# Seven block products in place of eight in the second layer's FFN input, from the ninth pair on

## What is computed

```
def swiglu(h, w_in, w_out):
    g, u = jnp.split(h @ w_in, 2, axis=-1)
    return (jax.nn.silu(g) * u) @ w_out
...
        fl = swiglu(rms_norm(xl, g_ffn_pre[i]) * (1.0 + sc2) + sh2, w_ffn_in[i], w_ffn_out[i])
        xl = xl + gt2 * rms_norm(fl, g_ffn_post[i])
```

## Time and profile before

| | us |
|---|---|
| median of 3 runs | 1643.54 (1643.48 to 1644.06) |
| the profiled execution, whole | 1640.58 |
| its span | 1638.8 |
| first half of the FFN input (11 pairs) | 1265.9 to 1391 |
| first half of the output product | 1391.4 to 1451 |
| second half of the FFN input (11 pairs) | 1451 to 1571 |
| second half of the output product and the end | 1571 to 1638.8 |

### The profile page before, as it was taken

One profiled execution on the slowest core, in us unless ns is written; L12 is line 12 of the kernel. 1 busy time (PEld: TensorE's weight loads), 2 busy tenths in 40 slices (PEclk: granted clock), 3 DMA queues, 4 the chain that ended last, 5 costly groups with the idle time before them and its releaser, 6 DMA issues.

```text
span 1638.8 us, 25486 instructions
## 1 busy us (share of the span) xinstructions
PE 1592.5 (97%) x9666; PEld 1362.3 (83%) x9666; DVE 871.4 (53%) x1488; ACT 684.6 (42%) x1289; POOL 413.8 (25%) x311
## 2 busy tenths in 40 slices
PE   6999999999899999999999999999999999999998
PEld 4878887678899999997887788888887888888886
DVE  5856567718888878868777420136845331011103
ACT  4242226827544444433336441248855322222322
POOL 2311232035000000000002242325433444444442
PEclk9999999999999999999999999999999999999999
DMA  9743111023244334438964536224012543333322
GB/s 358 268 132 90 40 27 53 2 78 90 84 138 143 123 118 143 123 126 292 352 252 143 167 120 139 80 86 106 15 67 62 173 123 100 107 102 91 99 95 76
DMA packets 176360, 204.07 MB, mean 125 GB/s; under 512 B 16664, under 2 KB 138864, under 8 KB 175856
## 3 DMA queue, kind: packets, MB, share of 16 engines
q1 hardware_dynamic: 162232, 156.62, 30.6%
q10 hardware_dynamic: 14008, 45.83, 8.8%
HBM read 187.97 MB, written 12.88 MB: 123 GB/s over the span
## 4 chain that ended last, share of the span: by engine, by line
PE 89%; DVE 4%; ACT 3%; DMA 1%; issue 1%; POOL 1%; SPq 0%; DVEq 0%; ACTq 0%; POOLq 0%
PE ps L2508 28%; PE ps L2555 25%; PE ps L3063 18%; PE ps L2875 3%; PE ps L2818 3%; PE ps L2781 3%; PE ps L2738 2%; PE ps L2664 1%; PE ps L2759 1%; PE ps L2625 1%; PE ps L2537 1%; DMA mod_early<-in_w_mod 1%; DVE prob L1837 1%; ACT junk L1153 1%; ACT prob L1337 1%
## 5 line engine op out<-in xcount | busy, mean ns | idle before, releaser
L641 POOL TENSOR_TENSOR w_lo<-w_raw,w_hi 128x1024 fp32r<-128x1024 f32 (+1 forms) x122 | 299.5, 2456 | 577.6 <-ACT w_hi L1166 577.6
L1166 ACT ACTIVATE w_hi<-w_raw 128x1024 fp32r<-128x1024 f32 (+1 forms) x202 | 211.9, 1051 | 193.9 <-PE ps L2555 166.3
L2508 PE MATMUL ps<-h_hi,w_hi 128*128 128x512 f32 (+1 forms) x768 | 254.9, 367 | 1.1 <-DVE h_lo L1714 1.1
L2508 PE MATMUL ps<-h_hi,w_lo 128*128 128x512 f32 (+1 forms) x768 | 252.9, 365 | 0.0
L2508 PE MATMUL ps<-h_lo,w_hi 128*128 128x512 f32 (+1 forms) x768 | 251.7, 363 | 0.0
L2508 PEld LDWEIGHTS ps<-h_hi,w_hi 128*128 128x128 f32 x768 | 133.8, 189 | 27.4 <-issue 2.1
L2508 PEld LDWEIGHTS ps<-h_lo,w_hi 128*128 128x128 f32 x768 | 133.2, 189 | 23.2
L2508 PEld LDWEIGHTS ps<-h_hi,w_lo 128*128 128x128 f32 x768 | 133.4, 189 | 22.9
L641 DVE TENSOR_TENSOR w_lo<-w_raw,w_hi 128x1024 fp32r<-128x1024 f32 x77 | 93.8, 1221 | 98.0 <-ACT w_hi L1166 97.8
L3063 PE MATMUL ps<-hc_hi,h_hi 128*128 128x384 f32 x420 | 141.7, 337 | 2.4 <-ACT x_u L1214 2.4
L3063 PE MATMUL ps<-hc_hi,h_lo 128*128 128x384 f32 x420 | 141.0, 336 | 0.0
(11 more groups left out here) (353 smaller groups left out, 3036.5 us busy)
## 6 DMA issues: line engine op xcount, KB each, us to landing
w_raw<-in_w_ffn_in SPq DMA_DIRECT2D x88, 512.0 KB, 3.8
w_raw<-in_w_ffn_out SPq DMA_DIRECT2D x66, 512.0 KB, 3.5
mod_raw<-in_w_mod ACTq DMA_DIRECT2D x38, 512.0 KB, 5.5
mod_early<-in_w_mod SPq DMA_DIRECT2D x30, 512.0 KB, 9.7
w_raw<-in_na_w_in SPq DMA_DIRECT2D x29, 512.0 KB, 3.7
gate_b<-in_w_mod ACTq DMA_DIRECT2D x18, 512.0 KB, 4.6
hid_far<-full SPq DMA_DIRECT2D x22, 384.0 KB, 2.3
xs<-hid_far SPq DMA_DIRECT2D x22, 256.0 KB, 6.0
```

Source lines behind the costliest of these rows:

```text
L641: eng.tensor_tensor(w_lo[:, ring(u), 0:width], w_raw[:, u % RAW, 0:width], w_hi[:, ring(u), 0:width].bitcast(F32), ALU.subtract).then_inc( ...
L1166: act.activation(w_hi[:, ring(u), 0:width], w_raw[:, u % RAW, 0:width], ACT.Copy).then_inc(w_hi_done, 1)
L2508: mm = pe.matmul(o[0], sta(x, o), mov(y, o), start=first and n == 0, stop=last and n == 2)
```

## The change

The first eight pairs of the first half stay as they are. Pairs 9 to 11 of the first half and all eleven of the second (14 pairs, numbered n = 0 to 13 in `QN`) are computed with seven products, each of 4 blocks of 128 features x 3 matmuls, with 256 columns moving. The tokens are split into two halves of 256 and the features into two halves of 512, which gives the activation blocks. What is new or moved:

- `quick_t_sums` makes the four sums of activation blocks (VectorE, during the first pair), from the unrounded activations, which now stay in `y_half` (`full_of`); `quick_t_high` and `quick_t_low` split them (pairs 2, 3, 6, 7).
- For each of the 14 pairs: `quick_sum` makes the four sums of weight blocks (VectorE, 512 columns each), `quick_high` (ScalarE) and `quick_low` (VectorE) split them two at a time (1,024 columns each), and the u unit's second block A22 alone is split as before: high part by ScalarE, low part by GpSimd, 512 columns. The g unit's low part moves to VectorE (`by_dve`), but for n = 0 and n = 3.
- `quick_product` on TensorE, in the order P5, P7, P2, P1, P3, P4, P6. P3 waits until ScalarE has copied P5's bank, P4 until VectorE has added P7's bank to that copy, P6 until VectorE has added P1's bank and the copy of P2's.
- `raw_free` holds back the load into a slot until the pair's last sum (S4) is made too.
- The multiplication silu(g) u writes `hid_raw1`; low parts of the hidden values are made after the stage's last pair (first half) or at its end (second half), since the output product needs them only then.
- Sums and plans of the last modulation vector come one pair earlier.

The core of the diff:

```diff
+    quick_g = [sp(("fi1L", half)) + 2 * j for half, j in QN]
+    quick_u = [g + 1 for g in quick_g]
+    for n, g in enumerate(quick_g):
+        if n not in (0, FH - QUICK):
+            by_dve[g] = True
...
+            if v in quick_g or v in quick_u:
+                eng.wait_ge(*quick_summed((quick_g if v in quick_g else quick_u).index(v), "s4"))
...
+            def quick_in(half, first, hooks):
+
+                s = sp(("fi1L", half))
+                for j in range(first, FH + 1):
+                    n = QN.index((half, first)) + j - first
+                    if j > first:
+                        d = quick_banks(n - 1)[2]
+                        dve.wait_ge(f_u, Q_U + n)
+                        dve.tensor_tensor(quad[:, QW:3 * QW].rearrange("p (a n) -> p a n", a=2), PS[:, d:d + 2, 0:QW],
+                                          bass.AP(q_u.tensor, q_u.offset, [list(q_u.ap[0]), [0, 2], [1, QW]]),
+                                          ALU.add).then_inc(f_12, 1)
+                        dve.tensor_tensor(quad[:, 3 * QW:], q_u, q_t, ALU.add).then_inc(f_22, 1)
+                    if j < FH:
+                        quick_low(n, 1)
+                    if j > first:
...
+                        dve.tensor_tensor(hid_raw1[:, (j - 1) * SEQ:j * SEQ], quad[:, 0:2 * QW], quad[:, 2 * QW:],
+                                          ALU.mult).then_inc(hid_made, 1)
+                    if j < FH:
+                        dve.wait_ge(s_used, Q_USED + 3 * n + 2)
+                        dve.wait_ge(fp_copied, Q_COPIED + 2 * n + 1)
+                        dve.tensor_tensor(q_t, quick_ps(quick_banks(n)[3]), q_part, ALU.add).then_inc(f_t, 1)
+                        feed(s + 2 * j + 1)
+                        if j + 1 < FH:
+                            quick_sum(dve, n + 1, "s1")
+                            quick_sum(dve, n + 1, "s3")
+                        dve.wait_ge(w_used, ring_no[s + 2 * j] + 1)
+                        dve.wait_ge(fp_copied, Q_COPIED + 2 * n + 2)
+                        dve.tensor_tensor(quad[:, 0:QW], quick_ps(quick_banks(n)[0]), q_two, ALU.add).then_inc(f_11, 1)
+                        if j + 1 < FH:
+                            quick_low(n + 1, 0)
+                            quick_sum(dve, n + 1, "s2")
+                            quick_sum(dve, n + 1, "s4")
+                        feed(s + 2 * j + 2)
...
+                for j in range(first, FH):
+                    n = QN.index((half, j))
+                    for p in (5, 7, 2, 1, 3, 4, 6):
+                        quick_product(n, p)
```

More of the change, by code:

```diff
@@ L53 @@
 PARTS = HALF // P
+QUICK = 8
+QN = [(0, j) for j in range(QUICK, FH)] + [(1, j) for j in range(FH)]
+QW = SEQ // 2
 FAST_JOBS = ("s1", "s3", "s4", "a22", "s2")
@@ L272, in build @@
         by_dve[u] = True
+    quick_g = [sp(("fi1L", half)) + 2 * j for half, j in QN]
[3 more added lines that the diff above has]
+            by_dve[g] = True
+    for half in range(2):
+        by_dve[sp(("fo1L", half))] = True
     ups = range(sp("fi0") + 3, sp("fi0") + 2 * FT, 2)
@@ L306, in build @@
         gate_b = sb("gate_b", [P, 2, D])
+        with ExitStack() as early:
+            s42 = sb("s42", [P, 2, UNIT], F32R, scope=early)
         xs = sb("xs", [P, 2, D])
+        with ExitStack() as early:
+            t4_lo = sb("t4_lo", [P, 4, QW], F32R, scope=early)
         full = sb("full", [P, KT, P])
@@ new lines, in unit_cols, with quick_banks, quick_ps, quick_slot @@
+        def unit_cols(u):
+            return slice(UNIT // 2 if u in quick_u else 0, unit_width(u))
+        def quick_banks(n):
+            return (0, 1, 4, 5) if n % 2 == 0 else (2, 3, 6, 7)
+        def quick_ps(bank):
+            return ps(bank, 0, QW)
+        def quick_slot(half, part):
+            n = ("s1", "s3", "s4", "s2").index(part)
+            return x_res[:, LT + n // 2, UNIT // 2 * (n % 2):UNIT // 2 * (n % 2 + 1)]
+        def quick_summed(n, part):
+            return w_summed, Q_SUMMED + 4 * n + ("s1", "s3", "s2", "s4").index(part) + 1
@@ new lines, in quick_sum @@
+        def quick_sum(eng, n, part):
+            g = quick_g[n]
+            a11, a12 = w_raw[:, g % RAW, 0:UNIT // 2], w_raw[:, g % RAW, UNIT // 2:]
+            a21, a22 = w_raw[:, (g + 1) % RAW, 0:UNIT // 2], w_raw[:, (g + 1) % RAW, UNIT // 2:]
+            s1, s3, s4, s2 = (quick_slot(n, x) for x in ("s1", "s3", "s4", "s2"))
+            if n:
+                done = quick_split(n - 1, 0 if part in ("s1", "s3") else 1)
+                eng.wait_ge(s_hi_done, done)
+                eng.wait_ge(s_lo_done, done)
+            if part == "s1":
+                for u in (g, g + 1):
+                    eng.wait_ge(landed[u % RAW], landed_value[u])
+                to, x, y, op = s1, a21, a22, ALU.add
+            elif part == "s3":
+                to, x, y, op = s3, a11, a21, ALU.subtract
+            elif part == "s2":
+                eng.wait_ge(*quick_summed(n, "s1"))
+                to, x, y, op = s2, s1, a11, ALU.subtract
+            else:
+                eng.wait_ge(*quick_summed(n, "s2"))
+                to, x, y, op = s4, a12, s2, ALU.subtract
+            eng.tensor_tensor(to, x, y, op).then_inc(w_summed, 1)
@@ L1309, in ffn_in, with quick_t_high, quick_high @@
                         mod_load(act, m)
+            def quick_t_high(t, done):
+                act.wait_ge(hc_summed, Q_TSUM + 4)
+                if t in (3, 4):
+                    act.wait_ge(mod_acc, sums_done(12 * KT - 1))
+                act.activation(quick_t[t][0], quick_t[t][2], ACT.Copy).then_inc(hc_hi_done, 1)
+            def quick_high(n, pair):
+                hi, _, raw = quick_place(pair)
+                act.wait_ge(*quick_summed(n, ("s3", "s4")[pair]))
+                quick_free(act, n, pair)
+                act.activation(hi, raw, ACT.Copy).then_inc(s_hi_done, 1)
```

211 lines of the change are left out of this document (181 added, 30 removed).

## The result

| | before | after |
|---|---|---|
| median of 4 runs, us | 1643.51 (1640.82 to 1644.06) | 1654.12 (1649.62 to 1654.69) |
| the profiled execution, whole | 1640.58 | 1654.39 |
| its span | 1638.8 | 1652.6 |

The ratio is 1.0064, 95% interval 1.0051 to 1.0078: **slower by 10.6 us**, where 1.3 were forecast. The time lies in the range, near its upper end. That is partly luck: the range reached so far only for the first rival's sake, and the first rival's steady price is not what made the kernel slow.

The account below looks back on a forecast made before the run. TensorE alone bounded the kernel; afterwards a ring of waits through the loads would. Second half +1.3, first half -0.3 and end +0.3 gave +1.3 on 1643.54, so 1644.8 us, range 1634 to 1657.

Parts of the forecast that it names:

- the first rival: Two loads issued in a row hold each other up, turns of 12.75 us, time 1658.2; chance 0.33 in full or part.
- The saving on TensorE: A pair's matmuls take 10.08 us in place of 10.88, 11.2 us over 14 pairs if TensorE never waits.
- The ring through the loads: S1 through S4, g low part and load landing (4.0) to the next S1: 10.3 us, 11.4 a pair with GpSimd.
- GpSimd's 1.07: GpSimd's low part of A22 goes ahead of VectorE's S2, which is written at 5.32 instead of 4.25.
- The second half, +1.3: Eleven pairs end at 121.0 us against 119.7 before, later pairs coming every 11.4 us.
- The end of the second half, +0.3: At the second output product: four early hidden low parts end before P6 does; the second tile may wait a little.
- The first half, -0.3: Its three new pairs, with the wait for P5's and P7's banks, take 32.3 us against 32.6 before.
- the extras at nothing: Activation sums and splits on VectorE, earlier modulation sums and similar were priced at zero; failing cover, TensorE waits 1 to 2 us once.
- 8.0 us of 10.08, so the total fits: VectorE's new work per pair, 8.0 us, was taken to fit within TensorE's 10.08 us pair.
- Rival 1: Same as the first rival: two loads in a row, landing 5.35 us in place of 4.0, time 1658.2; chance 0.33.
- Rival 2: GpSimd's low part finds a VectorE gap or follows S4, turn 10.3 us or less, time 1633.9; chance 0.22.
- What would show it: TensorE waiting before P5 and P2, S2 lasting 1.6 to 1.9 us; wrong if landing exceeds 4.2 or stalls sit elsewhere.

Follow-up runs that it names:

- e2: Changed kernel with A22's low part made by VectorE, not GpSimd, for all pairs but the first of each half; median 1636.8 us, ratio 0.9967.
- e5: e2 with only the first of four early hidden low parts left before the last pair's two-bank sum; median 1632.6 us, ratio 0.9946.
- e9: Repeat, for its trace, of the changed kernel with ScalarE rounding A22 and the g unit only after S4 and S2; 1643.5 us, one run.
- e3: Changed kernel with the second half's hidden low parts made one a pair, before S1; median 1646.3 us, ratio 1.0018.
- e1: Changed kernel with VectorE making the next pair's g low part before S1, not behind S4; median 1644.65 us, ratio 1.0014.
- e10: The kernel of e9 plus e1's edit (g low part before S1), against the changed kernel; median 1642.1 us, ratio 1.0003.

## Why the prediction was off

- **The saving on TensorE (11.2 us if unimpeded): right.** In e2, e5 and e9 the eleven pairs take 110.9 us plus at most 0.3, 8.5 less than before.
- **The ring through the loads, 11.4: right in its parts and its sum** (11.41 in e3). GpSimd's 1.07 in it measured 1.09. The prediction's GpSimd start (2.9 behind S1) was 2.99. GpSimd had asked while VectorE was busy, and went next in every turn. In the turn above its instruction of 1508.57 stands against VectorE's low part until 1509.23 and ends at 1510.38; S2, asked for at 1509.14 while GpSimd worked, ends 0.54 later, after 1.78 us in place of 0.69 (1.77 to 1.79 in the other turns). That GpSimd is served first there is read from these rows.
- **The second half, +1.3: measured +4.24; a term mis-sized.** 1.9 are the two late landings, which the prediction's 4.0 left out although it quoted a landing of 5.4 from the same kind of load. 0.7 lie at the start: the third pair's S1 came 15.9 us into the half, not 15.2. There ScalarE rounds a g unit (from 1459.32, for 1.05 us) in front of the sums, and VectorE's low part of them starts at 6.8 in place of 6.3. The rest of 0.3 is spread over the other turns.
- **The end of the second half, +0.3: measured +6.46; this step failed.** "VectorE's four early low parts of hidden values end before P6 does" priced four instructions at 0.6. The prediction had what it needed, the exclusion in the earlier trace rows (3.23 us in place of 1.28), and applied it to the ring alone. Here GpSimd makes two low parts of 1,024 columns in the same window, and the four took 6.85 us. Two thirds of the miss are the wait; the rest is the half clock behind it, which had no term at all.
- **The first half, -0.3: the number agrees (-0.38), by luck.** The three pairs took 32.68 us against 32.64 before: no gain, where 0.3 were forecast. The parts were right in kind (the end at 31.1 for the forecast's 30.9 or 31.0, then the wait for P5's and P7's banks, 1.56 from matmul to matmul for 1.3). The -0.4 lies in the first eight pairs, 93.8 us against 94.2 (126.86 less three pairs of 10.88), for which nothing was forecast; in the ten traces of the changed kernel and its variants they take 93.5 to 94.1. So the extras at nothing cost nothing.
- **"8.0 us of 10.08, so the total fits": too weak.** It was not what bound the changed kernel, but it was next. The round is 8.0 plus 1.4 of waits inside it, plus 1.1 for GpSimd: 10.5 (e1, e10), over TensorE's 10.08.
- **Rival 1 (two loads in a row):** fell as a steady price. Outside the two late turns, the first of two landed in 3.8 to 4.1 us, only the second after 5.0 to 5.3. The time it gave, 1658.2, was nearer than mine, for another reason. **Rival 2 (GpSimd in a gap):** it is what e9 built, and its turn of 10.3 was right (10.23). **What would show it:** the two waits a pair, S2's length and the load as releaser all stood where they were said to. Two of the signs of being wrong came too: the two late landings are over 4.2 us, and TensorE stood before P6 behind each of them, and again at the exit.

## What to carry to other kernels

When a faster scheme gives a helper engine a long round, add up the round with its waits, not the busy time, and write down every ring separately: after the first is shortened, the second binds. What an instruction costs that excludes another engine's depended here on its place: GpSimd's 512 columns added 1.1 us to a turn in front of S2 (11.41 in e3), left a turn of 10.23 behind S4, where VectorE would wait anyway (e9), and one of 10.50 where VectorE had no wait for a load left (e10). So try it first where that engine would wait anyway. And look at the exit of a stage in the same way as at its middle: here the next stage's helpers started as the last results were due, four low parts took 6.85 us in place of 2.4, and the 3.8 us that TensorE waited cost another 2.4 at a granted clock of 0.50.

## What the runs showed of the hardware that was not expected

- A wait of 3.8 us on TensorE was followed by 4.8 us at a granted clock of 0.50; one of 3.0 us by 3.1 us at 0.50 in e2 and by 5.7 in e9. After the wait of 1.56 us at the first half's exit the granted clock stayed at 1.00, in all nine traces that have it.
- Both late landings of a u unit (4.79 us for the load issued at 1500.66, 4.99 for 1535.90) have an instruction fetch of 16 KB within 1.2 us of the issue, on the queue for instructions. The other seven have none there. The fetches of the two begin 0.97 and 1.15 us behind the issue. Loads and fetches from 1500.6 to 1505.5 in the kernel after:

```profile
q1 hardware_dynamic: 2009, 1.02, 74.3%
q8 instruction: 1, 0.02, 1.5%
```

  Counting from 1380 us on, in the eleven traces four loads of a weight unit, with no other load within 3.6 us ahead, have a fetch that begins 0.97 to 1.15 us behind their issue, and all four landed after 4.8 to 5.0 us: these two, e1's one late landing (4.96 us, issued at 1540.74), and one of the kernel before (4.92 us, issued at 1438.99). With a fetch 0.4 to 0.8 us behind, the landing took 3.8 to 4.4 us; with one that began up to 0.6 us ahead, at most 4.04 (e1's load of 1498.74: 3.95), and with one 0.94 behind, 3.84 (e10's of 1473.80). Two landings of 4.8 and 4.9 us have no fetch within 2.6 us (the changed kernel's at 1571.10, e9's at 1558.68). So in these traces a fetch at that distance goes with a late landing, but isn't the only thing that does; that it delays the load is inferred, and was not tried by itself.
- At the exit, where VectorE and GpSimd each had instructions of two inputs one behind the other, they ended in turns, one instruction each (GpSimd 1579.77, VectorE 1580.32, GpSimd 1582.52, VectorE 1583.07): VectorE's third and fourth low part at the exit lasted 2.8 to 2.9 us for 0.6 us of work, GpSimd's two 2.7 and 2.8 for 2.4. VectorE, whose instructions were the short ones, lost 2.2 to 2.3 us on each, GpSimd 0.3 to 0.4.
